# A 64-byte tile moved to another place in the list of SBUF tiles, in a three-block float32 transformer kernel

## The reference, cut to what matters

```python
hdn = jnp.square(jax.nn.relu(rms_norm(x, pre_mlp_g[l]) @ w_up[l]))   # 1024 -> 4096
x = x + rms_norm(hdn @ w_down[l], post_mlp_g[l])                     # 4096 -> 1024
```

## Time and profile before

| | |
|---|---|
| median of 3 runs | 1420.99 us (1419.34 to 1423.31) |
| the profiled execution's own time | 1419.34 us |
| its span, from the first to the last instruction | 1417.5 us |
| mean granted TensorE clock | 0.98 |
| TensorE matmul busy | 1335.4 us, 94% |
| VectorE, ScalarE, GpSimd busy | 58%, 47%, 6% |

### The profile page before, as it was taken

One profiled execution on the slowest core, in us unless ns is written; L12 is line 12 of the kernel. 1 busy time (PEld: TensorE's weight loads), 2 busy tenths in 40 slices (PEclk: granted clock), 3 DMA queues, 4 the chain that ended last, 5 costly groups with the idle time before them and its releaser, 6 DMA issues.

```text
span 1417.5 us, 23851 instructions
## 1 busy us (share of the span) xinstructions
PE 1335.4 (94%) x10479; PEld 1284.0 (91%) x10479; DVE 826.5 (58%) x874; ACT 661.6 (47%) x934; POOL 88.2 (6%) x65
## 2 busy tenths in 40 slices
PE   4998989999999999898999999999989998899998
PEld 3987988989999999798898999998888897899998
DVE  5467436566653475743665665447848766666542
ACT  4354435455544444543544554434455544455432
POOL 3000002020000000000201000001100100000000
PEclk8999999999999999999999999999989999999999
DMA  6724234334655543414434365655343132356553
GB/s 192 228 74 149 88 122 149 119 119 141 205 191 190 186 120 93 146 54 157 149 94 145 120 209 183 204 182 152 115 139 120 40 110 89 100 173 204 179 198 100
DMA packets 195574, 202.94 MB, mean 143 GB/s; under 512 B 5716, under 2 KB 191847, under 8 KB 195471
## 3 DMA queue, kind: packets, MB, share of 16 engines
q1 hardware_dynamic: 192704, 194.82, 42.9%
q0 software_dynamic: 2464, 5.99, 1.4%
q10 hardware_dynamic: 303, 0.61, 0.1%
HBM read 200.33 MB, written 3.16 MB: 144 GB/s over the span
## 4 chain that ended last, share of the span: by engine, by line
PE 75%; DVE 11%; ACT 8%; issue 3%; DMA 2%; POOL 0%; ACTq 0%; DVEq 0%; POOLq 0%
PE bank L561 13%; PE bank L562 13%; PE bank L563 13%; PE bank L2085 6%; PE bank L2083 6%; PE bank L2087 6%; DVE w_lo L525 4%; ACT w_hi L515 3%; PE bank L602 2%; PE bank L604 2%; PE bank L603 2%; DVE head_sq L1547 1%; PE bank L1945 1%; PE bank L1976 1%; PE bank L1923 1%
## 5 line engine op out<-in xcount | busy, mean ns | idle before, releaser
L525 DVE TENSOR_TENSOR w_lo<-raw,w_hi 128x2048 fp32r<-128x2048 f32 (+7 forms) x210 | 424.1, 2030 | 426.4 <-ACT w_hi L515 426.1
L515 ACT ACTIVATE w_hi<-raw 128x2048 fp32r<-128x2048 f32 (+7 forms) x210 | 354.8, 1704 | 447.5 <-PE bank L563 169.9
L561 PE MATMUL bank<-act_hi,w_hi 128*128 128x256 f32 x1096 | 308.6, 282 | 0.0
L562 PE MATMUL bank<-act_lo,w_hi 128*128 128x256 f32 x1096 | 306.8, 280 | 0.0
L563 PE MATMUL bank<-act_hi,w_lo 128*128 128x256 f32 x1096 | 305.9, 279 | 0.0
L2083 PE MATMUL bank<-h_hi,w_hi 128*128 128x256 f32 x768 | 212.2, 276 | 0.0
L2085 PE MATMUL bank<-h_lo,w_hi 128*128 128x256 f32 x768 | 212.0, 276 | 0.0
L2087 PE MATMUL bank<-h_hi,w_lo 128*128 128x256 f32 x768 | 212.0, 276 | 0.0
L561 PEld LDWEIGHTS bank<-act_hi,w_hi 128*128 128x128 f32 x1096 | 206.1, 188 | 0.6 <-DVE act_lo L1764 0.3
L562 PEld LDWEIGHTS bank<-act_lo,w_hi 128*128 128x128 f32 x1096 | 205.8, 188 | 0.3
L563 PEld LDWEIGHTS bank<-act_hi,w_lo 128*128 128x128 f32 x1096 | 205.0, 187 | 0.0
(11 more groups left out here) (333 smaller groups left out, 2249.7 us busy)
## 6 DMA issues: line engine op xcount, KB each, us to landing
raw<-in_w_up_dram SPq DMA_DIRECT2D x32, 1024.0 KB, 5.5
raw<-in_w_down_dram SPq DMA_DIRECT2D x32, 1024.0 KB, 5.0
raw<-in_w_ff_dram SPq DMA_DIRECT2D x32, 1024.0 KB, 5.3
raw<-in_w_in_dram SPq DMA_DIRECT2D x23, 1024.0 KB, 5.4
raw<-in_w_xk_dram SPq DMA_DIRECT2D x8, 1024.0 KB, 5.6
raw<-in_w_xv_dram SPq DMA_DIRECT2D x8, 1024.0 KB, 5.0
raw<-in_w_mix_out_dram SPq DMA_DIRECT2D x8, 1024.0 KB, 5.0
raw<-in_w_xq_dram SPq DMA_DIRECT2D x8, 1024.0 KB, 4.9
```

The source lines that it names most:

```text
L515: ins = act.activation(d, r, ACT.Copy)
L525: ins = dve.tensor_tensor(d, r, h.bitcast(F32), ALU.subtract)
L561: pe.matmul(o, stat_hi, mov_hi, start=first, stop=False)
L562: pe.matmul(o, stat_hi, mov_lo, start=False, stop=False)
```

## The change

The allocation of `small` moves from between `x_t` and `act_hi` to between `row_inv` and `qk_dil`. No instruction, wait, size or order is changed. All tiles from `act_hi` to `row_inv` come to lie 64 bytes lower; everything before `small` and everything from `qk_dil` on stays where it is. `act_hi` is then 57344 bytes, exactly 56 x 1024, from the start of `w_hi`.

```diff
         x_t = sb("x_t", [P, KD, T])
-        small = sb("small", [P, 16])
         act_hi = sb("act_hi", [P, KD, T], F32R)
...
         row_inv = sb("row_inv", [P, 48])
+        small = sb("small", [P, 16])
         qk_dil = sb("qk_dil", [P, KD, T])
```

## The result

The changed kernel takes 1431.88 us, median of 7 runs (1430.21 to 1434.37), against 1423.31 us, median of 7 (1418.51 to 1426.52), for the kernel before. The ratio is 1.0063, with a 95% interval of 1.0046 to 1.0080: slower by more than the 0.3% that can be told from no change, by some 9 us. The profiled execution of the changed kernel took 1432.31 us with a span of 1430.5 us, 13.0 us longer than the span of before. The execution of before that was profiled lies 4 us under the median of its seven runs, so part of these 13 us is chance.

A forecast was written before the change was run, and what follows sets the result against it. TensorE's pace through its products was taken to bound the kernel. Profiled 1419.34 us + 0 + 0 + 0 + 0 = 1419.3, plus 1.65 to reach the median, gave 1421.0 us; range 1399 to 1438.

The forecast's parts named there:

- What bounds the kernel: Whole kernel: TensorE's pace through its products sets the end, with 75% of the chain; transfers hardly matter.
- Small tile, other engines, transfers, each at 0: Moved `small`, VectorE, ScalarE and GpSimd on shifted tiles, and DMA: 0 each; other engines bounded by -0.5 and +0.5 us.
- one of its own signs: VectorE's or ScalarE's means on `act_hi` and `act_lo` moving over 10 ns would show the other-engines term wrong.
- TensorE's products with `act`: 4,992 wide matmuls with `act`: value taken 0, bounds -20 and +23 us.
- an argument by neighbourhood: For `act` products: new position lies between two slow ones, 64 behind and 64 ahead of the grid, so change 0.
- rival 2: `act` on the grid of `w_hi`: load and stream get in each other's way; 1444 us, at half 1432; chance 0.26.
- one more step: Upper bound for `act` products: 4.4 ns more on each of 4,992 matmuls, +22.0 us.
- The fast stretches that are lost: Some 270 `act` products now at the fast pace would lose it: 270 x 4.4 = 1.2 us.
- The rule on the ports: Skill page's independent SBUF read ports for load and moving operand: relative tile place can't matter, `act` term 0.
- A rhythm taken up after a wait and then kept: TensorE's products: a load and stream rhythm, 117.7 or 113.4 ns, taken up on restarting after a wait, then kept.
- the profiled execution's standing among three: Profiled execution of before was the lowest of three, their median 1.65 us higher; so 1.65 us was added.

The follow-up runs named there:

- e11_break_one: Kernel before plus one extra triple of products, reading 640 bytes further on, at the second slab of each of three up-projections; ratio to before 1.0034.
- e3_h_on_grid: Kernel before with 320 unused bytes ahead of the late tiles, so `h` and `o` lie at offset 0, `act` still at 64; ratio to before 1.0125.
- e2: Changed kernel with two small tables moved ahead of `act_hi`, so `act` lies at offset 704, like `h`; ratio to before 1.0045.
- e9: Kernel before plus two extra triples of products, reading 640 bytes further on, at the second slab of each of three up-projections; ratio to before 1.0030.
- e12: Changed kernel with `neg_max` moved ahead of `act_hi`, so `act` lies at offset 192, `h` and `o` at 704; ratio to before 1.0065.
- e8: Kernel before with three small tables moved between `act_hi` and `act_lo`, so `act_hi` lies at 64 and `act_lo` at 704; ratio to before 1.0024.
- e10_break_up_after: Changed kernel plus two extra triples of products, reading at 640, at the second slab of each of three up-projections; ratio to before 1.0077.

## Where the prediction was right and where it failed, step by step

**What bounds the kernel.** Right: the chain is 76% TensorE, and a change of TensorE's pace went through to the end almost whole, 11.8 us of distances in 13.0 us of span.

**Small tile, other engines, transfers, each at 0.** Right in its value, though one of its own signs was crossed. The means on `mem_t` moved by 0 ns, and the busy time of ScalarE and VectorE by 0.2 us. But `act_lo` from `x_t` moved by 70 ns, where more than 10 was to show the term wrong. The group in before, in the kernel after and in e11_break_one:

```profile
L1287 DVE SCALAR_TENSOR_TENSOR act_lo<-x_t,g_cur,act_hi 128x256 fp32r<-128x256 f32 x32 | 16.3, 547 | 0.7 <-ACT act_hi L835 0.7
```

```profile
L1287 DVE SCALAR_TENSOR_TENSOR act_lo<-x_t,g_cur,act_hi 128x256 fp32r<-128x256 f32 x32 | 14.0, 477 | 0.7 <-ACT act_hi L835 0.7
```

```profile
L1292 DVE SCALAR_TENSOR_TENSOR act_lo<-x_t,g_cur,act_hi 128x256 fp32r<-128x256 f32 x32 | 14.0, 478 | 0.7 <-ACT act_hi L840 0.7
```

e11 has the tiles where before has them, and 478 ns all the same, so the place isn't the cause. In before 30 of the 32 took 472 to 489 ns, and two took 1525, each while a GpSimd addition of 2793 ns ran. The count was low, too: 96 instructions of each kind write `act_hi` and `act_lo`, not 64, so the bound should have been 0.8 us. DMA is 2% of the chain in both.

**TensorE's products with `act`.** Here is the step that failed: "the value I take is 0". The term was +11.8 us. The argument was that the new position lies between two that both have the slow pace, 64 behind the grid and 64 ahead of it, and so must have it too. The runs showed in its place that the offset does not work smoothly: in the long stretch 0, 32, 64, 96 and 128 give 120.0, 116.7, 117.7, 120.0 and 118.6. Between such values nothing can be interpolated. It was called an argument by neighbourhood and no more; the consequence, that the forecast at 0 had nothing better to stand on than the rivals, wasn't drawn. The time of 1431.88 us lies between the 1399 and 1438 of the stated range, but in the part that was there for rival 2; the forecast itself, 1421.0, was 10.9 us low.

**Rival 2 is what happened.** Its place is right (`act` exactly on the grid of `w_hi`), its sign is right, and so are its signs in the profile: 661 in 79 us is 652 in 78, below 660, with starts 0.12 apart throughout, while `h` kept 113.4. It was priced at one more step of 4.4 ns for each of 4,992 products, or half of it, 1432 us. The measured step is 120.0 - 117.7 = 2.3 ns, half of that, and the median is 1431.88. That the half price meets it so closely is luck: half a step was a guess with no row behind it, and it added 11 us to a base of 1421.0, where the medians show 8.6 us on 1423.3. With the distances of the table it is 9.3 us for `act` moving, 2.3 for `act` stationary, where the mean went from 117.0 to 119.8, and 0.2 for `o`. The fast stretches that are lost were 254 products against the 270 that I counted. What I held against this rival, that the trace has no third pace, was no argument: no wide float32r product of the kernel before lay at that offset, so no third pace could show. Of the mechanism, that load and stream get in each other's way, no run shows more than the longer distances.

**The rule on the ports.** The Trainium skill, page "TensorE: Matmul & The Clock Gate", section "Step-by-step: what each phase is for", has two independent read ports, from which I drew that no offset could matter. The runs disagree with that: with one tile of 320 bytes more and no other edit e3_h_on_grid is slower by 1.25%. Whether the ports themselves are the cause, no run shows. The same page, section "Wait — 56ns, not 53.3ns?", gives back-to-back matmuls one column per cycle and some 2.5 ns; for 256 columns my estimate from that is 109.2 ns. No wide float32r product with its own weight load came under 113.3 here over a stretch.

**A rhythm taken up after a wait and then kept.** Right in the main. At 64 a stretch is fast or slow for long, and 704 and 192 keep what they are given: with `act` at 704 or 192 the untouched `h` became slow (117.7 and 117.8 against 113.4), and in e2 it was fast again behind the gap in the third block. The break without a wait came with the position, not with tile or data, since in e9 the same tile read 640 bytes further on did it. But not every change of position breaks the slow rhythm: from 192 to 704 it stays (e12), with 64 and 704 in turns within each triple it stays (e8), and at 64 the fast one doesn't outlive the break (e9, e11). At 0 there is nearly one rhythm alone: 3,938 of 4,089 distances are 120 ns.

**Profiled time and median.** The forecast added 1.65 us for the profiled execution's standing among three. Among seven runs it stood 4.0 us under their median. By medians the change costs 8.6 us, with an interval of some 6.5 to 11.4, by distances 11.8. The 3 us between them are not settled; the third block's clock, which differs from execution to execution, is as large.

**What stays open.** Why TensorE needs 272, 282 to 283 or 288 cycles of its upper clock for the same load and stream (113.3, 117.7 and 120.0 ns x 2.4) is not shown, nor why 96 is as slow as 0 and 32 isn't. Only the activation tiles were moved. A kernel with `w_hi` and `w_lo` moved along with them would tell whether place against the weights or place in the partition counts; it wasn't run. Whether banks of the output take part wasn't tried either.

## What to carry to other kernels

In a kernel whose end is set by products with a weight load of their own, the order in which tiles are declared can cost about 1%. Here it cost up to 1.25%, and no layout tried was faster than the one of before. Measure the distance between starts, stretch by stretch, before and after any edit that moves an operand. If one kind of product is slower than another of the same shape, compare where their tiles lie against each other, and what ran just before; read each stretch by itself, since a mean over all of them can mix two paces. A value for a position that no product of the trace has can't be read off its neighbours; hold it open and measure it.

## What the runs showed of the hardware that wasn't expected

- The distance between starts of a 128x128 load with a 128x256 float32r stream, at granted clock 1.00, depends on where the moving tile lies, given here past a multiple of 1024 bytes from the stationary one: 120.0 ns at 0, for `act` as for `h`; 116.7 or 117.8 at 32; 120.0 at 96; some 118.6 at 128; 113.3 or 117.7 at 64, 192 and 704.
- At 192 and 704 which of the two it is was inherited from the products before: `h` at 113.4 behind `act` at 64 or 0, at 117.7 behind `act` at 704 or 192, in the first two blocks and up to a gap of 0.2 us in the third.
- The record of the weight load is longer too at offset 0: 192 ns against 188, for `act` in the kernel after and for `h` in e3.
- TensorE's granted clock over the same stretch of the last block, 1000:1112 us, was 0.92 in one kernel and 0.85 in another that up to there differs from it only by 12 added products, the last of them about 200 us earlier. In the opening, too, it differs, and the product that reads `small` shows it. Its spread by tile in the kernel after, and the window around it, where before has 696 ns as the median:

```profile
L1911 PE MATMUL bank<-cst,small x2: 1019/1038/1057, 23.8 to 24.6; 33*8 33x512 f32 x2
```

```profile
20.00:26.00 6.00, 6.00 (x21) 3.75 (x20) 4.53 (x8) 4.73 (x9) 2.64 (x2) 0.50 0.00 0
```

That product took 1.5 times as long at granted clock 0.50; in before the same window has 0.71. It is the clock and not the tile's new place that made it longer: e11_break_one has the tile at its old place and the same durations at granted clock 0.50, and e10_break_up_after has it at the new place and 591 ns as the median at 1.00. The row in e11_break_one:

```profile
L1916 PE MATMUL bank<-cst,small x2: 1019/1038/1057, 23.5 to 24.3; 33*8 33x512 f32 x2
```
